# The rotary heads of a decoder block: twenty projection jobs in the wide form, with an addition ahead of the rotation

## What is computed

```
h = rms_norm(x, g_mix)
q, k, v = h @ w_in            # 16 heads of 128 each: 4 of type A, 6 of B, 6 of C
A: rotary q and k, causal softmax attention
B: stick-breaking attention, no positions
C: rotary q and k, three dilated causal patterns, mixed by their softmax denominators
rotary: (x1, x2) -> (x1*cos - x2*sin, x2*cos + x1*sin)
```

## Time and profile before

| | |
|---|---|
| median of 3 runs | 1214.16 us (1213.57 to 1214.18) |
| the profiled execution, its own time | 1214.26 us |
| its span, first to last instruction | 1212.5 us |
| PE busy | 1193.7 us, 98% of the span |
| DVE busy | 797.9 us, 66% |
| ACT busy | 605.0 us, 50% |
| POOL busy | 172.4 us, 14% |
| granted TensorE clock | 0.998 of full speed |

### The profile page before, as it was taken

How to read it: one execution, slowest core, us unless ns; L and a number is a source line. 1 busy time by engine, 2 the same in 40 slices (tenths; PEclk the granted TensorE clock), 3 DMA queues, 4 the chain that set the end, 5 groups by cost and what they waited for, 6 DMA issues and landing times.

```text
span 1212.5 us, 20150 instructions
## 1 busy us (share of the span) xinstructions
PE 1193.7 (98%) x7164; PEld 1057.0 (87%) x7164; DVE 797.9 (66%) x1085; ACT 605.0 (50%) x897; POOL 172.4 (14%) x176
## 2 busy tenths in 40 slices
PE   8999999999999999999999999999999999999996
PEld 6888899999989889888888888888888888888885
DVE  7658866686667867666655666655666655666654
ACT  6345545555645657555433555433555333555442
POOL 8306500030323404100000000000000000000342
PEclk9999999999999999999999999999999999999999
DMA  9574554344544543455545545554454555455541
GB/s 355 215 274 171 193 183 151 138 158 154 221 166 172 176 170 140 171 191 192 208 176 196 179 176 193 198 197 175 174 204 175 206 187 194 173 179 204 201 142 69
DMA packets 33011, 224.25 MB, mean 185 GB/s; under 512 B 3793, under 2 KB 4177, under 8 KB 7121
## 3 DMA queue, kind: packets, MB, share of 16 engines
q1 hardware_dynamic: 32256, 220.22, 50.2%
q10 hardware_dynamic: 720, 3.59, 0.8%
HBM read 221.69 MB, written 2.10 MB: 185 GB/s over the span
## 4 chain that ended last, share of the span: by engine, by line
PE 92%; DVE 5%; ACT 1%; POOL 1%; issue 1%; DMA 0%; DVEq 0%; SPq 0%; ACTq 0%; POOLq 0%
PE bank L1023 23%; PE bank L1020 23%; PE bank L1021 23%; PE bank L1025 4%; PE bank L1027 4%; PE bank L1026 4%; PE bank L1066 3%; PE bank L1067 2%; PE bank L1068 2%; DVE w_low L673 2%; DVE part_a L718 1%; DVE part_a L883 1%; PE extra L1083 1%; DMA staged<-in_wv 0%; POOL acc L302 0%
## 5 line engine op out<-in xcount | busy, mean ns | idle before, releaser
L673 DVE TENSOR_TENSOR w_low<-staged,w_high 128x1024 fp32r<-128x1024 f32 x407 | 508.0, 1263 | 212.3 <-ACT w_high L364 207.5
L364 ACT ACTIVATE w_high<-staged 128x1024 fp32r<-128x1024 f32 x400 | 414.8, 1054 | 332.9 <-PE bank L1023 239.8
L1021 PEld LDWEIGHTS bank<-part_a,w_low 128*128 128x128 f32 x1408 | 264.7, 188 | 61.9
L1020 PE MATMUL bank<-part_a,w_high 128*128 128x512 f32 x704 | 279.7, 397 | 0.0
L1023 PE MATMUL bank<-part_a,w_high 128*128 128x512 f32 x704 | 278.5, 396 | 0.0
L1021 PE MATMUL bank<-part_a,w_low 128*128 128x256 f32 x1408 | 276.6, 278 | 0.0
L1021 PEld LDWEIGHTS bank<-part_b,w_low 128*128 128x128 f32 x1024 | 192.5, 188 | 45.3
L1023 PE MATMUL bank<-part_b,w_high 128*128 128x512 f32 x512 | 202.5, 396 | 0.0
L1020 PE MATMUL bank<-part_b,w_high 128*128 128x512 f32 x512 | 202.3, 395 | 0.0
L1021 PE MATMUL bank<-part_b,w_low 128*128 128x256 f32 x1024 | 201.1, 278 | 0.0
L1020 PEld LDWEIGHTS bank<-part_a,w_high 128*128 128x128 f32 x704 | 133.7, 190 | 0.2
(11 more groups left out here) (153 smaller groups left out, 1205.1 us busy)
## 6 DMA issues: line engine op xcount, KB each, us to landing
staged<-in_wup SPq DMA_DIRECT2D x64, 1024.0 KB, 4.8
staged<-in_wdown SPq DMA_DIRECT2D x64, 1024.0 KB, 4.8
staged<-in_wqk SPq DMA_DIRECT2D x32, 1024.0 KB, 4.8
staged<-in_wv SPq DMA_DIRECT2D x12, 1024.0 KB, 4.9
staged<-in_wbc SPq DMA_DIRECT2D x8, 1024.0 KB, 4.8
staged<-in_wmk SPq DMA_DIRECT2D x4, 1024.0 KB, 4.8
staged<-in_woa SPq DMA_DIRECT2D x4, 1024.0 KB, 4.8
staged<-in_wcq SPq DMA_DIRECT2D x4, 1024.0 KB, 5.1
```

The costliest lines, as they stand in the source:

```text
L364: nc.scalar.activation(w_high[:, job % 2, cols], staged[:, job % 4, cols], ACT.Copy).then_inc(high_ready, 1)
L673: tt(w_low[:, job % 2, cols], staged[:, job % 4, cols], f32(w_high[:, job % 2, cols]), ALU.subtract).then_inc(low_ready, 1)
L1020: mm(out[:, :], high, both, start=first, stop=False)
L1021: last = mm(out[:, 0:T], low, part[:, slot(kt), 0, :], start=False, stop=False)
```

## The change

The jobs of C and A become wide. As the bank now holds two halves to be added, `turn` first copies the right half to `spare[:, 1]`; `roped` adds the left half to it in place; `turn` waits for that and copies the exchanged halves from `spare[:, 1]`, no longer from the bank; `roped` multiplies from `spare[:, 1]`. Two semaphores are new. Nothing else moves.

```diff
-            def turn(off, job, n_out):
+            def turn(off, job, n_turn, n_out):
                 act.wait_ge(half_done, off(2) + (2 * job + 2))
                 act.wait_ge(taken, off(1) + (BANKS + n_out))
-                src = bank[job % 4]
-                nc.scalar.activation(spare[0:64, 0, :], src[64:P, 0:T], ACT.Copy)
-                nc.scalar.activation(spare[64:P, 0, :], src[0:64, 0:T], ACT.Copy).then_inc(turned, 1)
+                nc.scalar.activation(spare[:, 1, :], bank[job % 4][:, T:2 * T], ACT.Copy).then_inc(rope_moved, 1)
+                act.wait_ge(rope_added, off(1) + (n_turn + 1))
+                nc.scalar.activation(spare[0:64, 0, :], spare[64:P, 1, :], ACT.Copy)
+                nc.scalar.activation(spare[64:P, 0, :], spare[0:64, 1, :], ACT.Copy).then_inc(turned, 1)
...
             def roped(off, slot, n_turn, n_out, job):
-                done(off, job)
-                src = bank[job % 4]
+                dve.wait_ge(rope_moved, off(1) + (n_turn + 1))
+                tt(spare[:, 1, :], spare[:, 1, :], bank[job % 4][:, 0:T], ALU.add).then_inc(rope_added, 1)
                 dve.wait_ge(turned, off(1) + (n_turn + 1))
-                tt(spare[:, 1, :], src[:, 0:T], rope[:, 0, :], ALU.mult).then_inc(rope_made, 1)
+                tt(spare[:, 1, :], spare[:, 1, :], rope[:, 0, :], ALU.mult).then_inc(rope_made, 1)
                 tt(spare[:, 0, :], spare[:, 0, :], rope[:, 1, :], ALU.mult).then_inc(rope_made, 1)
...
-                    job_of(by(i), JOB_C + s, OUT_C + s, part_a, wide=False)
+                    job_of(by(i), JOB_C + s, OUT_C + s, part_a)
...
-                    job_of(by(i), JOB_A + s, OUT_A + s, part_a, wide=False)
+                    job_of(by(i), JOB_A + s, OUT_A + s, part_a)
```

More of the change, by code:

```diff
@@ L177, in build @@
         turned, rope_made = sem("turned"), sem("rope_made")
+        rope_moved, rope_added = sem("rope_moved"), sem("rope_added")
         held_ready, s_ready, t_ready, o_ready, o_taken = (
@@ L464, in _ @@
                     split(by(i), JOB_C + s + 2, 0)
-                    turn(by(i), JOB_C + s, OUT_C + s)
+                    turn(by(i), JOB_C + s, s, OUT_C + s)
                     if s == 1:
@@ L487, in _ @@
                     split(by(i), JOB_A + s + 2, 0)
-                    turn(by(i), JOB_A + s, OUT_A + s)
+                    turn(by(i), JOB_A + s, 2 * HEADS_C + s, OUT_A + s)
                     if s == 1:
```

## The result

| | before | changed |
|---|---|---|
| median | 1214.18 us (5 runs, 1213.57 to 1214.91) | 1220.81 us (5 runs, 1219.09 to 1221.46) |
| ratio, 95% interval | | 1.0053 (1.0041 to 1.0064) |
| profiled execution, its own time | 1214.26 us | 1219.09 us |
| its span | 1212.5 us | 1217.3 us |
| granted TensorE clock | 0.998 | 0.998 |

The change costs 0.5%: +6.6 us by the medians. In the profiled execution it is +4.8 us, the sum said +5.1. The other four executions of the changed kernel took 1220.7 to 1221.5 at a mean clock of 0.995 or 0.996, and lift the median by another 1.7; that part had no place in the sum. (The +6.6 that the prediction worked out from the matmul rule agrees with the medians by chance: experiment 2 shows that the wide jobs gain more than that rule gives, and experiments 5 and 11 that the 1.7 are the clock.)

The account below looks back on a forecast made before the run. PE was taken to bound the kernel (92% of the chain of waits). Terms: -3.8 (jobs) + 2.7 (C) + 1.2 (scores in A) + 3.7 + 1.3 (transposes) = +5.1 us, 1219.3 to 1219.4; range 1214.0 to 1223.0, the forecast's own 1218 to 1221.5.

Parts of the forecast that it names:

- the matmul rule: A warm matmul takes columns / 2.4 GHz plus some 2.5 ns: 0.04 us gained a job, sum some +6.6.
- The jobs: On PE in C and A, each of 20 wide jobs takes 5.57 us, 0.19 less: 3.8 us gained.
- The longer rotation: On ACT and DVE, two hand-overs and dependent copies make the step 0.92 us longer when DVE is free at once.
- Coupling: DVE late at D holds ACT until D + 1.30; in A's first iteration the exponential starts 4.5 us later.
- the waits of C: PE ahead of line 1137 in C: new idle time of 0.9 us in each of three iterations, 2.7 in all.
- the transposes: PE in A waits for the exponentials' chain: 3.7 us new idle time in the first iteration, 1.3 in the second.
- the scores in A: PE in A's first iteration waits 1.2 us for DVE's hold: 2.1 us of lateness against 0.9 of slack.
- All hidden, and faster: Rival: the longer rotation costs under 0.25 us in C and nothing in A; 3.8 us less, 1210.4. Chance 7%.
- Partly covered: Rival: cheaper copies, C waits half as long, lateness misses the hold; +0.6 us, 1214.8, no change to tell. Chance 13%.
- The lateness stops in C: Rival: DVE is in time for the hold, A's first iteration pays only coupling and POOL; +3.3 us, 1217.5. Chance 20%.
- It piles up: Rival: copies take 0.15 us more each, C's chains lose at two places, A's first iteration 1.5; +8 to +9, 1223. Chance 12%.
- the hidden places: In C, lateness stays hidden by 0.5 us before the outputs and 0.6 before the next hold.

Follow-up runs that it names:

- experiment 2: The changed kernel with only the wide jobs, keeping the old rotation and leaving out the low-part product in the rotary heads: 1211.76 us, ratio 0.9977.
- experiment 5: The changed kernel with three matmuls of constants on PE inside the wait for the transposes in stage A: 1219.27 us, ratio 1.0043.
- experiment 11: The changed kernel profiled once more, no edit: 1222.32 us at a clock of 0.994.
- experiment 7: The changed kernel with the attention's work of job 1 moved ahead of the rotation in stage A only: 1214.57 us, ratio 1.0001.
- experiment 4: The changed kernel with the attention's work of job 1 moved ahead of the rotation in both stages, C and A: 1210.56 us, ratio 0.9968.
- experiment 6: The changed kernel with the attention's work of job 1 moved ahead of the rotation in stage C only: 1216.82 us, ratio 1.0020.
- experiment 9: The changed kernel with ACT making one copy only, and DVE making the exchanged halves and the sum: 1215.67 us, ratio 1.0014.
- experiment 3: The changed kernel with narrow jobs, so only the longer rotation; q and k of the rotary heads come out doubled: 1222.90 us, ratio 1.0069.
- experiment 10: The changed kernel with job 1's attention work ahead of the rotation in both stages, and a rotation without the way back to ACT: 1214.20 us, ratio 0.9994.
- experiment 8: The kernel before, narrow jobs and old rotation, with job 1's attention work ahead of the rotation in both stages: 1213.49 us, ratio 0.9992.

## Why the prediction was right, point by point

**The jobs.** Forecast 5.57 a job, 0.19 less than before, 3.8 in all. The matmuls within a job of the changed kernel have the distances of B's, but from one piece of attention work to the next a job is 0.17 to 0.18 shorter, 3.5 in all, and experiment 2 shows -2.7 by the medians, with 3.4 forecast for it. So the term is a little too large. The 0.1 that the matmuls of line 1137 take more in each iteration of C was not forecast; it shows in the changed kernel and in experiments 2 and 7, not in 4, 6 and 9, where the exponentials come early. Why was not traced.

**The longer rotation.** 0.42, 0.46 and two copies of 0.42: the trace has 209.20, the first exchanged copy 0.88 behind, the second 0.42 behind that, and the exponentials 1.75 behind the first copy, 0.96 longer than the 0.79 of before. The forecast was 0.92.

**Coupling.** DVE late at D holds ACT. Shown by the profile (ACT idle for 2.26 ahead of 269.31), by experiment 3 (the rotation alone costs 7.2 us at full clock), and by experiments 4 and 9, which get at it in two different ways. Work moved out from behind the rotation takes away the waits of C and of the transposes; a rotation that no longer waits on ACT takes away those of C and most of the transposes' second (0.41 is left), and shortens the first from 3.20 to 2.03, though it makes a longer one at the hold.

**The waits, one by one**, each as the row's idle time plus 0.17 for the last matmul's overhang: C 3 x 0.95 = 2.9 (forecast 2.7); the scores in A 1.04 + 0.17 = 1.2 (1.2); the transposes 3.20 + 0.17 = 3.4 (4.1) and 1.57 + 0.17 = 1.7 (1.75), less 2 x 0.45 of before. With the jobs as forecast that would be -3.8 + 2.9 + 1.2 + 3.4 + 1.7 - 0.9 = +4.5. The waits' term that was mis-sized is the first iteration of A, by 0.7. I had 9.5 us of DVE's work from the split to the next rotation, plus 1.38: 10.9. It took 268.86 - 258.38 = 10.5, since POOL stood in DVE's way about as often as before and not more. And DVE was less late at the hold: it began the split ahead of it at 254.64, 3.17 before ACT's first copy of the next rotation (257.81), where 2.1 us of lateness would have left 2.9. Experiment 6 adds that the late hold, which I had made part of this term, doesn't lengthen it: PE's scores are late with it. Two signs that the prediction named came out smaller with it: PE is idle ahead of the transposes by 3.2 and 1.6 and not by 4 and 1.7, and the exponentials of A's first iteration come 3.5 - 0.8 = 2.7 later behind job 1's end and not over 3.

**The sum, iteration by iteration.** PE's matmuls for the outputs close each iteration, at 195.13 and 222.53 before. The next three before:

```profile
249.94 0.60 PE L1083 MATMUL extra<-x 128*128 128x256 f32 x2
277.73 0.60 PE L1083 MATMUL extra<-x 128*128 128x256 f32 x2
306.16 0.60 PE L1083 MATMUL extra<-x 128*128 128x256 f32 x2
```

and in the changed kernel:

```profile
222.89 0.59 PE L1086 MATMUL extra<-x 128*128 128x256 f32 x2
250.63 0.59 PE L1086 MATMUL extra<-x 128*128 128x256 f32 x2
281.93 0.59 PE L1086 MATMUL extra<-x 128*128 128x256 f32 x2
310.97 0.59 PE L1086 MATMUL extra<-x 128*128 128x256 f32 x2
```

An iteration of C takes 27.74 instead of 27.41, +0.33, where the forecast's terms give 0.9 - 4 x 0.19 = +0.14. The first of A takes 31.30 instead of 27.79, +3.5 (forecast 1.2 + 3.7 - 0.76 = +4.1), the second 29.04 instead of 28.43, +0.6 (forecast +0.5). Together 3 x 0.33 + 3.5 + 0.6 = +5.1, the forecast to the tenth; but that is luck in part, as C costs 0.6 more than forecast and A's first iteration 0.6 less. The profiles differ by 4.8 only, because the changed kernel's came to stage C some 0.3 us earlier, for reasons ahead of the change.

**The clock.** Not in the forecast at all. The sum was made in the time of one profiled execution, and no row of the kernel before holds a fall, as no wait there is long enough. In 9 of the changed kernel's 12 executions it fell and cost some 1.5 to 3 us. Experiment 11 shows it right behind the transposes' wait and nowhere else, and experiment 5 supports the cause: a shorter idle stretch, everything else in place, and the median is where the sum had it. That 1220.8 still lies in the forecast's own 1218 to 1221.5, and in the range up to 1223.0, is luck as far as these 1.7 us go: the room above 1219.3 was there for other reasons (longer copies, the pile-up).

**The rivals.** *All hidden, and faster*, falls by the three waits. *Partly covered*: too. *The lateness stops in C*: no, PE waited 1.2 for the hold. *It piles up*: the hidden places held, with no wait ahead of C's outputs or in C's holds.

## What to carry to other kernels

Where an edit adds a step that goes over to another engine and back, cost it at the place where that other engine is busiest, not by the step's length: what stands behind the step on the first engine now waits for the second one's queue. Put the work that PE waits for ahead of such a step where its inputs allow; here that alone turned a loss of 0.5% into a gain of 0.3%. And look for what an earlier end releases: experiment 10 freed ACT sooner, and thereby POOL, and was 3.6 us slower than experiment 4. Last, when a sum comes out right, compare it stage by stage too: here two misses of 0.6 us cancelled.

## What the runs showed of the hardware

**An idle stretch of PE can cost more than its length.** With a longest wait of 3.2 us in a kernel kept dense elsewhere, the clock fell in 9 of 12 executions (changed kernel) and 7 of 11 (experiment 6); with 2.9 in 4 of 5 (experiment 3); with 2.4 in 8 of 11 (experiment 10) and 9 of 11 (experiment 9, which has one of 2.0 too); with 1.9 in 1 of 5 (experiment 5); never in experiments 2, 4, 7 and 8, 39 executions, where no wait in these stages is over 1.06. In the changed kernel the fall costs some 1.5 to 3 us, and is what spreads its times. In experiment 9 its price varies: of the nine executions with a lower clock four took 1216.6 to 1217.1 and five 1215.1 to 1215.8, no more than the two at 0.998 (1215.5 and 1215.7). Its profiled execution, 1216.57, was still at 1.00 behind the hold's wait of 2.41, and at 0.50 from 274 to 276, behind the transposes' wait of 2.03; experiment 10's was at 0.50 behind a wait of 2.42. So the same idle time brings the clock down in one execution and not in another. Where the clock fell in the five cheap ones no profile shows. (The Trainium skill, TensorE: Matmul & The Clock Gate, What's actually happening, has the chip throttle the clock behind idle time and let it go again under work; the trace agrees, with 0.50 behind 3.22 us.)

**The same columns take less time in fewer matmuls.** 768 columns take 3 x 0.120 = 0.360 us as three matmuls and 5.57 / 16 = 0.348 as two, 0.19 us over the 16 tiles of a job, 0.17 to 0.18 from one piece of attention work to the next; experiment 2 times it. What of that is the weight load was not tried.
